# Stage ends, residual and norm by token tile in a two-block transformer kernel, with the last feed-forward pieces reordered

## What is computed

```python
h = x
# first block
h = h + even_mixer(rms_norm(h, ln_mix[0]))        # recurrent half and windowed attention half
h = h + swiglu(rms_norm(h, ln_ffn[0]))            # d_ff 2816
h = h + gated_deltanet(rms_norm(h, ln_mix[1]))
h = h + moe_swiglu(rms_norm(h, ln_ffn[1]))        # 8 experts, top 2, d_ff 3584
# second block, for l in 0, 1
x = x + 0.5 * swiglu_ffn(rms_norm_2(x, ffn1_norm[l]))
x = x + mixer(rms_norm_2(x, mix_norm[l]))         # two convolutions and a spatial gate
x = x + 0.5 * swiglu_ffn(rms_norm_2(x, ffn2_norm[l]))
return rms_norm_2(x, final_norm)

def rms_norm(x, g):
    return x * lax.rsqrt(jnp.mean(x * x, axis=-1, keepdims=True) + EPS) * g
def swiglu(h, w_gate, w_up, w_down):
    return (jax.nn.silu(h @ w_gate) * (h @ w_up)) @ w_down
```

## Time and profile before

| | |
|---|---|
| median of 3 runs | 2889.73 us (2888.15 to 2890.3) |
| span of the profiled execution, first to last instruction | 2887.0 us |
| its own time outside of that span | not recorded; the median is 2.7 us above the span |
| PE busy | 2600.4 us, 90% |
| DVE busy | 1777.1 us, 62% |
| ACT busy | 1242.4 us, 43% |
| DMA | 601.34 MB, mean 208 GB/s |
| mean granted clock of TensorE | 0.946 of full speed |

### The profile page before, as it was taken

The page is one execution under the profiler, slowest core; times in us unless marked ns, Lnnn a source line. Parts: engine busy times, 40 slices in busy tenths (PEclk is TensorE's granted clock), DMA queues, the critical chain, the costliest instruction groups (busy, mean ns, idle before and its releaser), DMA issues.

```text
span 2887.0 us, 36005 instructions
## 1 busy us (share of the span) xinstructions
PE 2600.4 (90%) x14026; PEld 2204.6 (76%) x14026; DVE 1777.1 (62%) x1749; ACT 1242.4 (43%) x1026; POOL 59.6 (2%) x35
## 2 busy tenths in 40 slices
PE   8699897677999999999999997998789989986997
PEld 6399785565778787878778786997569979964996
DVE  4455344443889898988888896553735445453553
ACT  2333201212667676767666675332133343311432
POOL 0000001210000000000000000000100000001000
PEclk9899998887999999999999998999899999998998
DMA  8255142002989898989999898552326565430453
GB/s 322 78 186 174 58 146 88 1 1 88 337 315 364 302 372 307 357 318 348 330 336 337 313 371 313 184 196 67 106 83 200 184 226 175 144 129 17 161 195 102
DMA packets 313146, 601.34 MB, mean 208 GB/s; under 512 B 6017, under 2 KB 130049, under 8 KB 312833
## 3 DMA queue, kind: packets, MB, share of 16 engines
q1 hardware_dynamic: 313088, 600.55, 58.7%
HBM read 599.48 MB, written 1.05 MB: 208 GB/s over the span
## 4 chain that ended last, share of the span: by engine, by line
PE 64%; DVE 7%; PEld 3%; DVEq 2%; issue 2%; ACT 2%; DMA 1%; PEldq 0%; ACTq 0%
PE bank L172 18%; PE bank L174 18%; PE bank L173 18%; PE bank L383 3%; PE bank L1757 2%; DVE scratch L1896 2%; DVE weights_lo L1665 2%; PE bank L1442 1%; DVEq L1897 1%; PE bank L1492 1%; PEld bank L174 1%; PEld bank L172 1%; PEld bank L173 1%; PE bank L1466 1%; DMA scratch<-in_ffn_w_gate 1%
## 5 line engine op out<-in xcount | busy, mean ns | idle before, releaser
L1665 DVE TENSOR_TENSOR weights_lo<-mslot,weights_hi 128x2048 fp32r<-128x2048 f32 x338 | 769.6, 2288 | 89.5 <-ACT weights_hi L1544 84.2
L1544 ACT ACTIVATE weights_hi<-mslot 128x2048 fp32r<-128x2048 f32 x338 | 646.4, 1918 | 256.2 <-PE bank L174 183.8
L481 DVE TENSOR_TENSOR weights_lo<-scratch,weights_hi 128x2048 fp32r<-128x2048 f32 x165 | 377.3, 2291 | 410.2 <-ACT weights_hi L474 407.4
L172 PE MATMUL bank<-x_hi,weights_hi 128*128 128x256 f32 x1760 | 504.6, 287 | 28.1 <-DVE x_lo L308 19.2
L173 PE MATMUL bank<-x_lo,weights_hi 128*128 128x256 f32 x1760 | 503.6, 286 | 0.0
L174 PE MATMUL bank<-x_hi,weights_lo 128*128 128x256 f32 x1760 | 503.4, 286 | 0.0
L474 ACT ACTIVATE weights_hi<-scratch 128x2048 fp32r<-128x2048 f32 x165 | 316.1, 1921 | 346.2 <-PE bank L174 304.0
L172 PE MATMUL bank<-weights_hi,x_hi 128*128 128x512 f32 x904 | 371.5, 411 | 32.6 <-DVE weights_lo L1665 32.6
L172 PEld LDWEIGHTS bank<-x_hi,weights_hi 128*128 128x128 f32 x1760 | 343.8, 195 | 31.9 <-DVE x_lo L308 20.9
L174 PE MATMUL bank<-weights_hi,x_lo 128*128 128x512 f32 x904 | 360.7, 399 | 0.0
L173 PE MATMUL bank<-weights_lo,x_hi 128*128 128x512 f32 x904 | 360.6, 399 | 0.0
(11 more groups left out here) (340 smaller groups left out, 2317.9 us busy)
## 6 DMA issues: line engine op xcount, KB each, us to landing
mslot<-in_o_moe_w_down SPq DMA_DIRECT2D x58, 2048.0 KB, 8.6
mslot<-in_o_moe_w_gate SPq DMA_DIRECT2D x57, 2048.0 KB, 8.9
mslot<-in_o_moe_w_up SPq DMA_DIRECT2D x57, 2048.0 KB, 9.0
scratch<-in_ffn_w_gate SPq DMA_DIRECT2D x44, 1024.0 KB, 7.1
scratch<-in_ffn_w_up SPq DMA_DIRECT2D x44, 1024.0 KB, 5.5
scratch<-in_ffn_w_down SPq DMA_DIRECT2D x44, 1024.0 KB, 5.0
mslot<-in_o_w_in SPq DMA_DIRECT2D x8, 2048.0 KB, 8.4
mslot<-in_w_in SPq DMA_DIRECT2D x10, 1536.0 KB, 10.0
```

What stands on the lines that cost most here:

```text
L172: pe.matmul(out, stationary[0], moving[0], start=start, stop=False)
L481: dve.tensor_tensor(m.wlo[i][:, :], m.fslot[i], m.whi[i][:, :], ALU.subtract).then_inc(m.sig["f_lo"], 1)
L1544: act.activation(m.whi[places[half]][:, :], raw[:, half * PIECE:(half + 1) * PIECE], ACT.Copy).then_inc(s["r_hi"], 1)
L1665: dve.tensor_tensor(m.wlo[places[half]][:, :], raw[:, half * PIECE:(half + 1) * PIECE], m.whi[places[half]][:, :], ALU.subtract).then_inc( ...
```

## The change

1. **Residual and norm by token tile.** The output projection goes tile 0 (both halves), then tile 1 (both halves). DVE adds tile 0, ACT takes its sum of squares and root, DVE scales it (`norm_scale`), and PE turns its eight squares between the two halves of tile 1. Tile 1's sum of squares is taken in halves on ACT, each as soon as that half is added. All squares are now ACT's, and the root's function table is loaded by an explicit `preload_act_table` ahead of the wait. Tile 1 is scaled half by DVE and half by ACT.
2. **The next stage begins with the first transposed piece.** PE waits for each of the eight pieces ahead of its first use (`xT_in`, and `n_xl` counted by piece). From u = 1 the transposes go to banks 2 to 5.
3. **Ahead of feed-forwards that follow a mixer** (u = 1, 6, 9) the first gate and up pieces are split between the two tiles' norms (`first_hi`, `first_lo`); ahead of the others (u = 4, 7) they stay where they were.
4. **The last feed-forward pieces.** The loop ends one unit earlier, and PE's order becomes gate(10), up(10), down(9) and down(10) of tile 0, then down(9) and down(10) of tile 1 half 0, then of half 1. The last hidden values go into the memory of x_hi and x_lo, the last down weights into the first weight buffer (`ffn_place`).
5. **The ends.** The input comes in two DMAs, one for each tile. The final gain is loaded after the last hidden values; scaling by norm and gain is one DVE instruction, and the output goes in three DMAs (tile 0, then two halves of tile 1).

```diff
+def add_residual(dve, m, t, half, psum, scale=None):
+    r = m.res[:, t, half * HALF:(half + 1) * HALF]
+    if scale is None:
+        last = dve.tensor_tensor(r, psum[:, :], r, ALU.add)
+    else:
+        last = dve.scalar_tensor_tensor(r, psum[:, :], scale, r, ALU.mult, ALU.add)
+    if not (t == 0 and half == 0):
+        last.then_inc(m.sig["n_res"], 1)
...
+EARLY = (1, 6, 9)
...
+def turned(m, u, k):
+    bank = k // 2 if u == 0 else 2 + k // 2
+    return m.ps[bank][:, (k % 2) * SEQ:(k % 2 + 1) * SEQ]
...
+def final_scale(dve, m, t, at, end):
     s = m.sig
+    if at == 0:
+        dve.wait_ge(s["n_sd"], 2 * LAST + t + 1)
+        dve.reciprocal(m.rstd[t], m.sd[t])
         dve.drain()
+        dve.wait_ge(s["final_in"], 16)
+    dve.scalar_tensor_tensor(m.xn[:, t, at:end], m.res[:, t, at:end], m.rstd[t], final_gain(m)[:, at:end],
+                             ALU.mult, ALU.mult).then_inc(s["out_ready"], 1)
+def norm_scale(dve, m, u, t):
+    dve.wait_ge(m.sig["n_sd"], 2 * u + t + 1)
+    dve.reciprocal(m.rstd[t], m.sd[t]).then_inc(m.sig["n_rstd"], 1)
+    dve.drain()
+    cols = slice(0, D) if t == 0 else slice(0, HALF)
+    dve.tensor_scalar(m.xn[:, t, cols], m.res[:, t, cols], m.rstd[t], None, ALU.mult).then_inc(m.sig["n_xn_d"], 1)
+def norm_dve(dve, m, u, gain, v=None):
+    s = m.sig
+    norm_scale(dve, m, u, 1)
+    early = u in EARLY
+    if v is not None:
+        if not early:
+            ffn_lo(dve, m, v, "gate", 0)
         for k in range(KT):
+            dve.wait_ge(s["n_xh"], KT // 2 * m.splits[u] + k // 2 + 1)
+            dve.scalar_tensor_tensor(m.xl[:, k, :], turned(m, u, k),
+                                     gain[:, k:k + 1], m.xh[:, k, :], ALU.mult, ALU.subtract).then_inc(s["n_xl"], 1)
+        if not early:
+            ffn_lo(dve, m, v, "up", 0)
         return
...
+def norm_stats(act, m, u, between=None):
     s = m.sig
+    act.preload_act_table(ACT.Sqrt)
     if u == 0:
+        act.wait_ge(s["eps_in"], 1)
+        act.wait_ge(s["x_in0"], 16)
     else:
+        act.wait_ge(s["n_res"], 3 * u - 2)
+    act.activation(m.xn[:, 0, :], m.res[:, 0, :], ACT.Square, accum_out=m.ss0)
+    act.drain()
+    act.activation(m.sd[0], m.ss0, ACT.Sqrt, scale=1.0 / D, bias=m.eps).then_inc(s["n_sd"], 1)
+    if between is not None:
+        between()
+    if u == 0:
+        act.wait_ge(s["x_in1"], 16)
+    else:
+        act.wait_ge(s["n_res"], 3 * u - 1)
+    act.activation(m.xn[:, 1, 0:HALF], m.res[:, 1, 0:HALF], ACT.Square, accum_out=m.ss1a)
+    act.drain()
+    act.activation(m.part1, m.ss1a, ACT.Copy, scale=1.0 / D, bias=EPS)
+    if u > 0:
+        act.wait_ge(s["n_res"], 3 * u)
+    act.activation(m.xn[:, 1, HALF:D], m.res[:, 1, HALF:D], ACT.Square, accum_out=m.ss1b)
+    act.drain()
+    act.activation(m.sd[1], m.ss1b, ACT.Sqrt, scale=1.0 / D, bias=m.part1).then_inc(s["n_sd"], 1)
+def norm_act(act, m, u, gain, v=None):
+    s = m.sig
+    early = u in EARLY
+    norm_stats(act, m, u, (lambda: first_hi(act, m, v)) if early else None)
+    act.wait_ge(s["n_rstd"], 2 * u + 2)
+    act.activation(m.xn[:, 1, HALF:D], m.res[:, 1, HALF:D], ACT.Copy, scale=m.rstd[1]).then_inc(s["n_xn_a"], 1)
+    if v is not None:
+        if not early:
+            ffn_hi(act, m, v, "gate", 0)
...
+def norm_pe(pe, m, u, t):
     s = m.sig
+    if u == 0 and t == 0:
         pe.wait_ge(s["ident_in"], 16)
+    pe.wait_ge(s["n_xn_d"], 2 * u + t + 1)
+    for k in range(KT):
+        if t == 1 and k == KT // 2:
+            pe.wait_ge(s["n_xn_a"], u + 1)
+        last = pe.transpose(turned(m, u, k)[:, t * P:(t + 1) * P], m.xn[:, t, k * P:(k + 1) * P], m.c["ident"])
+        if t == 1 and k % 2 == 1:
+            last.then_inc(s["n_tr"], 1)
+def xT_in(pe, m, u, k):
+    n = u - sum(i < u for i in m.splits)
+    side = "n_xT_d" if k // 2 % 2 == 0 else "n_xT_a"
+    pe.wait_ge(m.sig[side], 4 * n + k // 4 * 2 + k % 2 + 1)
...
+def out_pe(pe, m, i, yT, u):
     s = m.sig
+    for t in range(NT):
+        for half in range(2):
+            if t == 0:
+                block_in(pe, m, i + half)
             for k in range(KT):
                 last = pe.matmul(m.ps[4 + 2 * t + half][:, :], yT[:, k, t * P:(t + 1) * P],
                                  mblock(m, i + half)[:, k, :], start=(k == 0), stop=(k == KT - 1))
@@ -386,39 +448,43 @@
                 last.then_inc(s[f"m_used{(i + half) % 4}"], 1)
             else:
                 last.then_inc(s["o_done"], 1)
+            if t == 1 and half == 0:
+                norm_pe(pe, m, u, 0)
+    norm_pe(pe, m, u, 1)
...
+def out_dve(dve, m, i, n, u, v=None):
     s = m.sig
     for half in range(2):
+        dve.wait_ge(s["o_done"], 2 * n + half + 1)
+        add_residual(dve, m, 0, half, m.ps[4 + half])
+    norm_scale(dve, m, u, 0)
+    if v is not None:
+        first_lo(dve, m, v)
+    for half in range(2):
+        block_used(dve, m, i + half)
+        add_residual(dve, m, 1, half, m.ps[6 + half])
...
-    def down(u, first=False, final=False):
-        split_in("down", NU - 1 if final else u)
+    def down_part(u, t, half, first, final):
+        hi, lo = parts(0 if final else KINDS["down"], D)
+        hh, hl = ffn_hidden(m, last=final)
+        cols, tok = slice(half * HALF, (half + 1) * HALF), slice(t * P, (t + 1) * P)
+        for k in range(FU // P):
+            last = split_product(pe, m.ps[4 + 2 * t + half][:, :], (hh[:, k, tok], hl[:, k, tok]),
+                                 (hi[:, k, cols], lo[:, k, cols]),
+                                 start=first and k == 0, stop=final and k == FU // P - 1)
+        return last
+    def down(u, first=False):
+        split_in("down", u)
         pe.wait_ge(s["f_h"], u + at + 1)
-        hi, lo = parts("down", D)
-        hh, hl = (t[:, :].rearrange("p (k t) -> p k t", t=SEQ) for t in (m.hh, m.hl))
-        for k in range(FU // P):
-            for t in range(NT):
-                for half in range(2):
-                    cols, tok = slice(half * HALF, (half + 1) * HALF), slice(t * P, (t + 1) * P)
-                    last = split_product(pe, m.ps[4 + 2 * t + half][:, :], (hh[:, k, tok], hl[:, k, tok]),
-                                         (hi[:, k, cols], lo[:, k, cols]),
-                                         start=first and k == 0, stop=final and k == FU // P - 1)
+        for t in range(NT):
+            for half in range(2):
+                last = down_part(u, t, half, first, False)
         last.then_inc(s["f_ddone"], 1)
     gate(0)
@@ -454,16 +526,56 @@
     gate(1)
     down(0, first=True)
     up(1)
-    with pe.Fori(2, NU) as u:
+    with pe.Fori(2, NU - 1) as u:
         gate(u)
         down(u - 1)
         up(u)
-    down(NU - 1, final=True)
+    gate(NU - 1)
+    up(NU - 1)
+    split_in("down", NU - 2)
+    pe.wait_ge(s["f_h"], at + NU - 1)
+    for half in range(2):
+        down_part(NU - 2, 0, half, False, False)
+    split_in("down", NU - 1)
+    pe.wait_ge(s["f_h"], at + NU)
+    for half in range(2):
+        down_part(NU - 1, 0, half, False, True).then_inc(s["f_out"], 1)
+    for half in range(2):
+        down_part(NU - 2, 1, half, False, False)
+        last = down_part(NU - 1, 1, half, False, True)
+        if half == 0:
+            last.then_inc(s["f_out"], 1)
+    last.then_inc(s["f_ddone"], 2)
+    if u_out is not None:
+        norm_pe(pe, m, u_out, 0)
+        norm_pe(pe, m, u_out, 1)
...
+def ffn_place(kind, u):
+    return 0 if kind == "down" and isinstance(u, int) and u == NU - 1 else KINDS[kind]
...
-    if not (v == 0 and isinstance(u, int) and u == 0):
+    if kind == "down" and isinstance(u, int) and u == NU - 1:
+        eng.wait_ge(m.sig["f_gdone"], v * NU + NU)
+    elif kind == "gate" and isinstance(u, int) and u == 0:
+        if v > 0:
+            eng.wait_ge(m.sig["f_ddone"], v * NU)
+    elif not (v == 0 and isinstance(u, int) and u == 0):
...
-    hidden(NU - 1)
+    hidden(NU - 1, last=True)
+    for half in range(2):
+        dve.wait_ge(s["f_out"], 3 * v + half + 1)
+        add_residual(dve, m, 0, half, m.ps[4 + half], scale)
+    if u_out == LAST:
+        final_scale(dve, m, 0, 0, D)
+    else:
+        norm_scale(dve, m, u_out, 0)
+    dve.wait_ge(s["f_out"], 3 * v + 3)
+    add_residual(dve, m, 1, 0, m.ps[6], scale)
     dve.wait_ge(s["f_ddone"], at + NU)
-    for t in range(NT):
-        for half in range(2):
-            r = m.res[:, t, half * HALF:(half + 1) * HALF]
-            last = dve.scalar_tensor_tensor(r, m.ps[4 + 2 * t + half][:, :], scale, r, ALU.mult, ALU.add)
-    last.then_inc(s["res_ready"], 1)
+    add_residual(dve, m, 1, 1, m.ps[7], scale)
...
-    dve.drain().then_inc(s["res_ready"], 1)
+    dve.drain().then_inc(s["n_res"], 3)
+    norm_scale(dve, m, 4, 0)
...
-            sp.dma_start(m.res, w["x"][0].rearrange("(t p) d -> p t d", p=P)).then_inc(s["x_in"], 16)
+            x = w["x"][0].rearrange("(t p) d -> p t d", p=P)
+            sp.dma_start(m.res[:, 0, :], x[:, 0, :]).then_inc(s["x_in0"], 16)
```

(8 more changed lines are left out.)

295 lines of the change are left out of this document (111 added, 184 removed).

## The result

The changed kernel takes 2811.0 us (median of four runs, 2805.3 to 2811.2), the kernel before 2888.9 (2886.8 to 2890.3): a ratio of 0.973, interval 0.9718 to 0.9742. That is 78 us where 66 were forecast. (Lines have moved: residual additions L290 and L292, norm L325 to L407, transposes L421, the split product L174 to L176, output projection L445.)

The account below looks back on a forecast made before the run. PE bounds the kernel (64% of the span), with serial stretches of 8.7 to 16.5 us at nine stage boundaries. Gains of 71.5 less 5.1 (clock) and 0.3 (start) give 66: 2824 us, range 2806 to 2847.

Parts of the forecast that it names:

- A to D: Boundaries: A mixer to feed-forward 17.4 us, B odd mixer to experts 3.5, C feed-forward to mixer 21.0, D feed-forward to feed-forward 6.2.
- A: Mixer to feed-forward (u=1, 6, 9): 6.0 us, transposes included, against 11.2, 12.1 and 12.1; 17.4 us gained.
- E: Experts to feed-forward (u=4): no gain, as ACT waits for gate(1), issued behind four mixer blocks.
- F: The last norm: last addition to end 7.0 us against 16.5, last store 3.1; 9.5 us gained.
- G: The start: no gain, PE's first matmul waits for its weight block; second x DMA loses 0 to 0.5 us.
- H: Last pieces of five feed-forwards: PE's waits for the last hidden values go, 10.7 us, and two clock dips, 3.2.
- The transposes of tile 0: Eight transposes between the two banks of tile 1, inside the projection: put at 1.0 us.
- The clock term: Low clock behind the shorter, mostly idle boundary stretches: three more dips of 1.6 to 1.7 us, 5.1 lost.
- Rival 2: Hand-overs cheaper than counted at eight boundaries (3) and the clock stays up (13): gain 82, 2808 us; chance 0.13.
- Rival 1: Clock eats a part: 6 us of low clock at each of eight boundaries, 24 lost, gain 47, 2843 us; chance 0.15.

Follow-up runs that it names:

- the kernel before with the shorter fills: The kernel before with unread matmuls, half as many as in a first try, put into PE's idle time at the boundaries: 2876.8 us, ratio 0.9965.

## Why the prediction was right, step by step

**The boundaries (A to D)** came out as built, 55.5 against 52.1 of stretch. The last addition to the first matmul was 4.6 (forecast 5.0) at u=1, 6 and 9, 3.7 (4.0 to 4.2) at u=2, 3, 5 and 8, 7.4 (7.7) at u=7. The excess of 3.4 is in hand-overs and pace, which I had rounded up. The experiments that undo one piece of A at a time move the stretches by 2.8 (early pieces) and 2.7 (first x_lo), the sizes of the steps.

**E** was right: nothing at u=4, since gate(1) waits behind four blocks. Only when that wait is taken away by moving the blocks does the stage gain, 11.8.

**F** was 10.6, not 9.5: the last stores took 2.1 us, under the 3.1 of my line. The line joined a store of 1024 KB (4.0) with a load of 512 KB (3.4); the store of 512 KB takes 2.6. By the fit in the Trainium skill's page "DMA: Bandwidth & Descriptors" ("Anatomy of one DMA — SWDGE (gpsimd) path") the last store would take 2.6, an estimate from its figures. The 2.6 measured for 512 KB and the 2.1 for 256 KB lie 0.6 and 0.5 under that fit.

**G** was right: the first matmul is not later (15.36 instead of 15.47). The first 64 take 22.5 us instead of the 20.9 of the earlier trace rows, but that is not the second DMA's doing: the three kernels made from the kernel before, with one DMA for the input, have 22.5, 22.9 and 23.1. The last of these (the kernel before with the shorter fills):

```profile
14.97 23.07 PE L640 MATMUL bank<-mslot,xT 128*128 128x512 f32 x64 [1.21 <-DMA mslot<-in_e_w_in]
```

So the profile of the kernel before was a good one at this place, and 1.6 us of the mixers' loss are no cost of the change.

**H** was right in mechanism and size: 15.0 in the feed-forwards with the changed starts against 13.9, and 18 (interval 11 to 20) when made alone. What the sum didn't have is that it also covers tile 0's norm: below the ends by token tile it is worth 26.

**The transposes of tile 0** cost 0.9 us in the projection, as estimated (8.48 + 6.13 against 2 x 6.87 between additions). The mixers lost another 4.7, 0.6 to 1.6 each and ahead of their output projection, which was not in the sum. Of these, 1.6 are the first 64 matmuls just named and 1.7 the longer low clock at the start of the odd mixer; the cause of the other 1.4 stays open.

**The clock term was wrong**, and it has the largest share in the 12 us by which the result is better than the forecast. I took one more dip for each of u=2, 5 and 8 (5.1 lost), because PE would find the low clock sooner behind a shorter stretch. One of the three came: the odd mixer behind u=2 starts with 10.2 us of matmuls at 0.50 and not 6.8, 1.7 lost. My rows showed the projections at u=5 and not the odd mixer, where the low clock was there already. Behind u=5 and 8 the projections run at 1.00, with a pause of 1.8 us between two groups of transposes ahead of them. That neither dip came is partly luck: with only u=1, 6 and 9 made different, the projections behind u=8 began with 3.4 us at 0.50, and with one more pause of 1.3 us ahead of them those behind u=5 and 8 began with 6.0 and 5.8 us. Instead the router and the first expert got more of the full clock, 15.5 us of matmuls at 0.50 where there were 29.8. From u=3's last addition to the first expert's last it takes 164.7 us instead of 174.5, of which the boundary is 5.1. This one repeats: the changed kernel's variants with the same boundary at u=3 and nothing added behind it have 164.2 to 165.6. It is 4.8 of the experts' 5.0.

Added up against the forecast: 3.4 (two dips that did not come) + 5.0 (experts) + 1.1 (F) + 3.4 (A to D) + 1.1 (H) + 0.4 (G) = 14.4, less 2.5 that the mixers lost beyond the forecast and the dip (1.6 at the start, 1.4 open, 0.5 regained on the transposes), is 11.9, the distance from 66 to 78. Rival 2 (2808) is 3 us from the result. Its two halves were cheaper hand-overs, 3, and 13 from the clock; measured are 3.4 and 8.4. Rival 1 asked for 6 us more of the low clock behind each of eight boundaries. In the first 14 us behind them there are 37 us at 0.50 in all, where the kernel before had 35, so it falls, though the low clock itself is still there at six of the eight. Filling the pauses that are left gives some 11 us at the boundaries and 15 in the experts, so the term is real in size.

The rule of the Trainium skill's page "TensorE: Matmul & The Clock Gate" ("A second HAM failure mode: psum-queue depth-cycling") that short idle times between groups make the clock swing comes out in part in the tails (two, four and five of five pauses of 2.1 us). Behind a pause of 1.8 us the changed kernel has the low clock at u=2 and none at u=5 and 8.
